# The second weight chunk between the modulation's two blocks, and two units begun on the first block

## The reference, cut to what matters

```python
c_act = jax.nn.silu(c)
for l in range(DEPTH):                                   # DEPTH = 2
    mod = c_act @ w_ada[l] + b_ada[l]                    # (1024) @ (1024, 3072)
    shift, scale, gate = jnp.split(mod, 3, axis=-1)
    h = rms_norm(x, norm_g[l]) * (1.0 + scale[:, None]) + shift[:, None]
    proj = h @ w_in[l]
    gq, gk, gv, glr, gz, dq, dk, dv, dz = split_columns(proj)
    gqkv = jax.nn.silu(causal_depthwise_conv(jnp.concatenate([gq, gk, gv], axis=-1), conv_w[l]))
    ...                                                  # two attention branches on these
    x = x + gate[:, None] * y
```

## Time and profile before

| | us |
|---|---|
| median of 3 runs (lowest, highest) | 1747.41 (1746.85, 1748.83) |
| the profiled execution | 1747.27 |
| its span | 1745.5 |
| PE busy | 1723.2 (99%) |
| ScalarE, VectorE, GpSimd busy | 672.0, 739.3, 732.1 |

### The profile page before, as it was taken

The page is one execution under the profiler, slowest core; times in us unless marked ns, Lnnn a source line. Parts: engine busy times, 40 slices in busy tenths (PEclk is TensorE's granted clock), DMA queues, the critical chain, the costliest instruction groups (busy, mean ns, idle before and its releaser), DMA issues.

```text
span 1745.5 us, 22025 instructions
## 1 busy us (share of the span) xinstructions
PE 1723.2 (99%) x8485; PEld 1407.4 (81%) x8485; DVE 739.3 (42%) x926; ACT 672.0 (38%) x871; POOL 732.1 (42%) x319
## 2 busy tenths in 40 slices
PE   6999999999999999999999999999999999999998
PEld 4677788777788888888889888888888888888887
DVE  4645765665766333332331634641113433333123
ACT  4444573544574433333333322232223333333223
POOL 1342226233225444444444444444444444444442
PEclk9999999999999999999999999999999999999999
DMA  9642115112113222222233322222222232222222
GB/s 356 236 145 97 49 49 217 49 73 97 49 49 116 101 96 96 96 89 78 90 105 111 109 95 96 96 97 97 96 96 96 75 115 96 98 97 75 85 98 82
DMA packets 34906, 180.75 MB, mean 104 GB/s; under 512 B 4470, under 2 KB 6652, under 8 KB 19356
## 3 DMA queue, kind: packets, MB, share of 16 engines
q1 hardware_dynamic: 28640, 161.50, 25.7%
q10 hardware_dynamic: 6204, 18.39, 2.9%
HBM read 177.78 MB, written 2.10 MB: 103 GB/s over the span
## 4 chain that ended last, share of the span: by engine, by line
issue 43%; PE 28%; POOL 25%; SPq 1%; DVE 1%; DMA 1%; ACT 1%; POOLq 0%; DVEq 0%; ACTq 0%
POOL wl_both L576 25%; PE ps L1123 4%; PE ps L1125 4%; PE ps L1124 4%; PE ps L1417 4%; PE ps L1419 3%; PE ps L1418 3%; SPq L521 1%; PE ps L1484 1%; PE ps L1458 1%; DMA ada_w<-w_ada 1%; PE ps L1259 1%; PE ps L1471 1%; PE ps L1495 0%; PE ps L1429 0%
## 5 line engine op out<-in xcount | busy, mean ns | idle before, releaser
L576 POOL TENSOR_TENSOR wl_both<-raw_both,wh_both 128x1024 fp32r<-128x1024 f32 (+1 forms) x256 | 609.5, 2401 | 733.4 <-ACT wh_both L668 731.0
L1123 PE MATMUL ps<-xh,wh_both 128*128 128x512 f32 x1280 | 503.1, 393 | 3.5 <-DVE xl L1956 1.6
L1125 PE MATMUL ps<-xh,wl_both 128*128 128x512 f32 x1280 | 498.4, 389 | 0.0
L1124 PE MATMUL ps<-xl,wh_both 128*128 128x512 f32 x1280 | 498.3, 389 | 0.0
L668 ACT ACTIVATE wh_both<-raw_both 128x2048 fp32r<-128x2048 f32 x127 | 243.4, 1916 | 494.4 <-PE ps L1125 484.3
L1123 PEld LDWEIGHTS ps<-xh,wh_both 128*128 128x128 f32 x1280 | 240.2, 188 | 65.9 <-issue 12.7
L1125 PEld LDWEIGHTS ps<-xh,wl_both 128*128 128x128 f32 x1280 | 240.2, 188 | 50.6
L1124 PEld LDWEIGHTS ps<-xl,wh_both 128*128 128x128 f32 x1280 | 240.4, 188 | 47.9
L598 POOL TENSOR_TENSOR wl_both<-raw_both,wh_both 128x1024 fp32r<-128x1024 f32 x46 | 113.3, 2477 | 238.9 <-ACT wh_both L823 167.0
L1123 PE MATMUL ps<-fh,wh_both 128*128 128x512 f32 (+1 forms) x374 | 141.2, 377 | 0.1
L1124 PE MATMUL ps<-fl,wh_both 128*128 128x512 f32 (+1 forms) x374 | 140.8, 376 | 0.0
(11 more groups left out here) (295 smaller groups left out, 2265.4 us busy)
## 6 DMA issues: line engine op xcount, KB each, us to landing
raw_both<-ffn_in_stream SPq DMA_DIRECT2D x44, 1024.0 KB, 4.7
raw_both<-mixer_stream SPq DMA_DIRECT2D x40, 1024.0 KB, 4.7
raw_both<-layer_stream SPq DMA_DIRECT2D x36, 1024.0 KB, 5.4
raw_both<-ffn_out_stream SPq DMA_DIRECT2D x32, 704.0 KB, 4.0
ada_late<-w_ada ACTq DMA_DIRECT2D x24, 512.0 KB, 4.5
ada_w<-w_ada SPq DMA_DIRECT2D x16, 512.0 KB, 12.2
gate_w<-w_ada ACTq DMA_DIRECT2D x4, 1024.0 KB, 11.4
x<-x_t SPq DMA_DIRECT2D x1, 2048.0 KB, 8.1
```

Of the source, the lines that this page charges most:

```text
L576: last = nc.gpsimd.tensor_tensor(wl[u][:, cols], raw[u][:, cols], wh[u][:, cols].bitcast(F32), ALU.subtract)
L1123: nc.tensor.matmul(bank_ap, w0, x0, start=first, stop=False)
L1124: nc.tensor.matmul(bank_ap, w0, x1, start=False, stop=False)
L1125: return nc.tensor.matmul(bank_ap, w1, x0, start=False, stop=last)
```

## The change

SP loads chunk 1 between block 0 and block 1 of the modulation, no longer after block 1. ScalarE takes chunk 1's high part after block 0's `xh`, no longer after block 1's, and issues `small_loads(1)` between the copy of block 1's rows and its `xh`, no longer after block 0's. PE runs unit 1 in the opening as well, in banks 2 and 7 (`SECOND_BANKS`): the slices 0 to 3 of both units stand between the tiles and transposes of block 1, the slices 4 to 7 of both behind them. Of the ten constant products around block 1's tiles (two, two and six) six remain, all ahead of unit 0. `late_tile(0)` waits until both banks of unit 1 are emptied, since bank 2 is its own; unit 2 waits for the banks of unit 0 instead of unit 1. ScalarE empties both tiles of unit 1 at its second quarter.

```diff
+SECOND_BANKS = (2, 7)
...
-            sp.dma_start(raw[1], ins["layer0_stream"][1]).then_inc(raw_landed[1], 16)
+                if b == 0:
+                    sp.dma_start(raw[1], ins["layer0_stream"][1]).then_inc(raw_landed[1], 16)
...
                         nc.scalar.activation(gate[:, b], ps[:, 4 + b], ACT.Copy).then_inc(rows_copied, 1)
+                        if b:
+                            small_loads(1)
...
                         if b == 0:
-                            small_loads(1)
-                        else:
                             take_high(first + 1)
...
-                    bank = ps[:, t]
+                    bank = ps[:, SECOND_BANKS[t] if (l, stage, j) == (0, "conv", 1) else t]
...
                         if kind in ("conv", "q"):
-                            if p % 2:
+                            if (l, kind, j) == (0, "conv", 1):
+                                for t in range(2 if p == 1 else 0):
+                                    empty(kind, j, t)
+                            elif p % 2:
                                 empty(kind, j, p // 2)
...
+            def second_steps(moving, low0, ks, tiles=(0, 1)):
+
+                for k in ks:
+                    pe.wait_ge(low_ready, low0 + k + 1)
+                    for t in tiles:
+                        if k == 0:
+                            half_ready(0, UNIT0["layer0"], 1, t)
+                        cols = slice((t * KT + k) * P, (t * KT + k + 1) * P)
+                        last = products(ps[:, SECOND_BANKS[t]], (wh[1][:, cols], wl[1][:, cols]),
+                                        (moving[0][:, k], moving[1][:, k]), k == 0, k == KT - 1)
+                        if k == KT - 1:
+                            last.then_inc(tile_done, 1)
...
                 pe.wait_ge(late_landed[buf], 16 * sum(loads))
+                if n == 0:
+                    pe.wait_ge(banks_free[1], emptied(1, 1))
...
                     ada_turn(0)
-                    constant_products(2)
-                    ada_tile(1, 0)
-                    constant_products(2)
+                    constant_products(6)
                     claim(0, unit0, 0)
                     chunk_ready(0, unit0, 0)
-                    first_steps(*first, range(0, 1))
+                    first_steps(*first, range(0, 2))
+                    ada_tile(1, 0)
+                    first_steps(*first, range(2, 4))
                     ada_tile(1, 1)
-                    first_steps(*first, range(1, 3))
+                    pe.wait_ge(mod_ready, 1)
+                    pe.wait_ge(xn_ready, KT)
+                    second_steps(*first, range(0, 4), (0,))
                     ada_tile(1, 2)
-                    first_steps(*first, range(3, 4), (0,))
                     ada_tile(1, 3)
-                    first_steps(*first, range(3, 4), (1,))
+                    second_steps(*first, range(0, 2), (1,))
                     ada_turn(1)
-                    constant_products(6)
+                    second_steps(*first, range(2, 4), (1,))
                     first_steps(*first, range(4, KT))
+                    second_steps(*first, range(4, KT))
...
+                    if (l, stage, j) == (0, "conv", 1):
+                        return
                     if stage in ("conv", "q"):
                         if half == 0:
-                            pe.wait_ge(banks_free[(unit - 1) % 2], emptied(unit - 1, t))
+                            emptied_by = unit - 2 if (l, stage, j) == (0, "conv", 2) else unit - 1
+                            pe.wait_ge(banks_free[emptied_by % 2], emptied(emptied_by, t))
```

## The result

The changed kernel takes 1753.21 us (median of 20 runs, 1749.84 to 1757.44), the kernel before 1747.61 (20 runs beside it, 1746.85 to 1749.18): a ratio of 1.0031, 95% interval 1.0025 to 1.0037. The forecast was 1749.6 with a range up to 1751.6; the change costs 5.6 us, not 2.2. The executions of the changed kernel don't scatter around one value, they lie in groups: one at 1749.84, 6 from 1750.3 to 1750.9, 3 from 1752.1 to 1752.4, 7 from 1754.0 to 1755.1, 3 from 1757.2 to 1757.4. The first profiled execution took 1752.20 us, 1750.5 of them its span.

A forecast was written before the change was run, and what follows sets the result against it. The prediction took TensorE, busy 99% of the span, as the bound. Unit 2 starting at 68.93 instead of 66.65 adds 2.3 us (1.6 gained by filling gaps, 3.85 paid for the wait) to 1747.27: 1749.6 us, range 1747.3 to 1751.6.

The forecast's parts named there:

- The timetable up to the stall: PE's opening, rebuilt from unit costs: first product at 27.78, `lr` at 56.24, 10.20 us later for 11.05 us of work.
- The moved transfer: Chunk 1 ahead of block 1 in SP's queue: 2.4 us delay per tile, costing nothing, with 1.7 us to spare.
- The wait and its price: PE behind `lr`, until ScalarE empties unit 1's banks: idle 3.85 us, whole kernel 2.3 us slower, 1749.6 us.
- the ledger's 68.93: Forecast start of unit 2 on PE: 63.96 plus late tiles and `gate`, against 66.65 before.
- where the ledger said 1.6: The same sum without PE's wait behind `lr`: 2.3 - 3.85, so 1.6 us faster than the kernel before.
- the clock falls in the new wait: Rival, PE's products behind the stall after `lr`: slow clock loses 1.75 us more, 1751.3 us; chance 0.18.
- the granted clock reads 9 in every slice: Argument from the profile before, tenths of full speed in every slice: speaks against any clock fall.
- this stretch is less than half as long: Argument against a clock fall: the 3.85 us stall compared with PE's idle stretch before 9.53 us.
- What PE does after about 70 us is untouched: PE's later work runs almost without gaps, so a shift at that point arrives whole at the end.
- Late load 4's slack: Load issued behind `gate`, landing at 77.2, asked for at 78.5: slack 1.3 us, nothing lost, up to 1 us possible.

The follow-up runs named there:

- the load alone: The kernel before with only chunk 1's load moved ahead of block 1's tiles in SP's queue: 1752.42 us, ratio 1.0025.
- the first trace of after: First profiled execution of the changed kernel, without any edit: 1752.20 us.
- The second extra trace: The changed kernel traced again without any edit, the second of two more traces: 1754.01 us.
- The other extra trace: The changed kernel traced again without any edit, the first of two more traces: 1756.52 us.
- the kernel with 32 calls: The changed kernel with 32 calls of the constant product, two products each, ahead of the first late tile's wait, filling 7.41 us: 1754.72 us, ratio 1.0041.
- those on banks 6 and 7: The changed kernel with unit 1 in banks 6 and 7, without the first late tile's wait: 1750.27 us; three kernels built further on it: 1748.64, 1746.70, 1744.79 us.
- the take of chunk 3 moved: The changed kernel with ScalarE's take of chunk 3's high part behind the copy of unit 1's second bank: 1750.25 us, ratio 1.0017.
- the second and third step: Banks 6 and 7, late load 2 early, plus block 1's last tiles earlier in the opening: 1746.70 us; besides, late load 4 right behind late load 3: 1744.79 us.
- the first step: The changed kernel with unit 1 in banks 6 and 7, no wait, and late load 2 issued with the first two, ahead of `lr`: 1748.64 us, ratio 1.0007.

## Why the prediction was wrong, by its own steps

**The timetable up to the stall: right.** First product 27.81 in the same timeline (27.78 forecast), block 1's transposes 42.02 (42.04), restart 45.12 (45.19) after 1.11 us of idle time (1.2), `lr` 56.13 (56.24), PE free 60.07 (60.11), stall 3.79 (3.85), end of the stall 63.86 (63.96). The moved transfer is hidden, no tile of block 1 waits; by the experiment on the load alone it is hidden by the products ahead of the tile, not by slack that was there: the prediction priced the delay at the last tile, and the one to price it at was the first.

**The wait and its price: right as a sum, in part by luck.** With the stall filled the kernel takes 1749.88, the forecast's 1749.6 within 0.3. Two errors nearly cancel in it: unit 2 starts at 68.50 there, 0.43 ahead of the ledger's 68.93, and late load 4 costs 0.74, which the sum had at nothing. With the wait removed and late load 2 issued early unit 2 starts 1.65 earlier than before, where the ledger said 1.6; here too the first product was 0.28 late with its x (28.06 against 27.78), so in the same timeline it is 1.9.

**The step that failed: the rival "the clock falls in the new wait", chance 0.18 and price 1.75 us.** The forecast put the clock's loss at nothing. It is the case in all three traced executions, and over the forecast it costs 1.1, 4.5 and 5.4 us in them (1.07, 1.07 + 3.4 and 1.07 + 4.31; 0.3 more each against the 1.92 us that the pair of late tiles takes at full clock). Which of the 20 executions have it is an estimate from their times and mean clocks; the sums of the three traces fit the groups so:

- 1749.6 + 1.07 (the loss in the first trace of after: unit 2 at 70.00, not 68.93) = 1750.7, near the group from 1750.3 to 1750.9. No trace of this group exists. Its mean granted clock is 0.998, and the traced execution with this loss has 0.999, so this sum may not be what happened in it.
- The same with the late chunk, 1.77 (5.14 - 3.37): 1752.4. The traced execution of 1752.20 is in that group; mean clock 0.999.
- 1749.6 + 1.07 + 3.4 = 1754.1. The second extra trace took 1754.01; the group of 7 has a mean clock of 0.996 to 0.997, so it too has a long stretch at half clock.
- 1749.6 + 1.07 + 4.31 (4.72 less the 0.41 ahead of the stall) + 1.4 for the chunk = 1756.4. The other extra trace took 1756.52; the last group, another 0.8 to 1.0 higher, has 0.994 to 0.995.
- The single execution at 1749.84 has a mean clock of 1.000 and lies at the forecast: without a fall, as far as its time and clock tell.

I set aside the clock on two grounds, and both were misread. First, "the granted clock reads 9 in every slice": a slice is 43.6 us, and 3.4 us at half clock leave 0.96 of it, which still prints as 9; that row could not speak against a fall. Nor could the windows at the start: where the constant products of the earlier trace rows are slow, from 9.5 us on, the granted clock of the kernel before reads 1.00 (11 products in this window, 19 of the same in the filled kernel's window from 60 to 62):

```profile
10.00:12.00 2.00, 2.00 (x11) 2.00 (x10) 1.61 (x3) 1.70 (x4) 0.00 (x0) 1.00 0.99 374
```

The pace was the better witness. Second, "this stretch is less than half as long" as the 9.5 us ahead of the first product: the runs show half clock behind idle times of 3.79, 3.74, 2.78, 2.45 and 1.99 us. (Not behind each of this size: waits of 1.78, 2.23 and 2.28 us, in the kernel with 32 calls and two of those on banks 6 and 7, have 1.00 in all windows behind them. And not only behind these: in two of the 14 traces the clock falls near 20 us behind 0.63 us. So the length of the last wait doesn't decide alone; what else does no run here shows.) And I priced the fall by one loss where it has a spread. (The loss itself was read a little high: 32 constant products take 3.84 us in this view, not 3.7, so 1.6 are lost in the earlier trace rows, not 1.75.)

That the fall at this place comes from the stall's idle time is shown from both sides: added alone to the kernel before, a stall of 3.74 us is followed by half clock and costs 5.9; filled with constant products it costs 3.6 (1751.09 against 1747.49), its length; filled in the changed kernel, it gives back 3.3 and shrinks the spread of the executions from 7.6 us to 1.4. How much of these medians is the clock and how much the late chunk is split in single traces only. The Trainium skill, "TensorE: Matmul & The Clock Gate", Part 1: The HAM clock gate, says that the slow state is the default and that an idle stretch brings back 1.2 GHz; the rows at 0.50 behind the stall in all three traces of the changed kernel agree, the three waits of 1.78 to 2.28 us named above don't show it, and the weight that the prediction gave to this rule was too small.

**The chunk near 540 us: not foreseen.** "What PE does after about 70 us is untouched" holds in the code. But the chunk that is awaited there lands 6.9 to 7.5 us after its issue instead of 4.8 (7.3 in the first trace of after), in 7 of the 14 traces of this study (this one of the changed kernel, its slower extra one, the load alone, the stall alone, and three of the four kernels on banks 6 and 7), and costs 1.4 to 1.8 us. In an eighth (the take of chunk 3 moved) it lands after 6.3 and PE doesn't wait for it. It goes neither with the fall of the clock behind a stall (two traces with such a fall lack it, two without one, those of the second and third step, have it) nor with a part of the change. None of the three traces with a filled stall has it; whether the filler keeps it away no run here shows. The one trace of the kernel before doesn't show it. Its cause stays open.

**Late load 4's slack.** I gave it 1.3 us by a landing of 4.5 us. With the stall filled its tile waits 0.74, and on banks 6 and 7 up to 2.28. The 4.5 is the median of single transfers, and a late load is two, issued one behind the other. With the stall filled the two are issued from 72.30 on and the tile starts at 78.92, 6.6 us later; in the first step it is 6.4 (70.64 to 77.00). So the term that was mis-sized is the landing of the whole load.

## What to carry to other kernels

A new wait on TensorE costs its own length, and then perhaps the clock: here the granted clock read 0.50 for 3 to 12 us behind waits of 1.99 to 3.79 us in seven traces, differently in each execution, and stayed at 1.00 behind waits of 2.23 and 2.28 in two others. So put work in a wait that is needed anyway, or constant products if there is none, or choose banks that need no wait; and look for the fall in windows of 1 or 2 us, since a page's slices hid 3.4 us of it. When PE's order is moved forward, move the loads behind it too, one by one, until no tile waits: here that, with two banks that need no wait and another order in the opening, made a loss of 5.6 us a gain of 3.0. And price a load of several transfers from its first issue to its last landing, not by one transfer's median.

## What was unexpected of the hardware

- Useless work made a kernel faster: 32 products of a constant, 3.84 us of them in a wait of that length, took 3.3 us off the median (a part of which can be the late chunk).
- The same program with the same stall of 3.79 us stays at half clock until about 67, 75 or 76 us in three executions.
- The granted clock reads 1.00 from 9.5 us on, while the first 32 constant products take 5.47 us instead of the 3.84 that 32 of them take at 60 us: at the start of the record the pace tells more than the clock's row.
- In two of the 14 traces the granted clock falls to 0.50 from about 20 to 23 us behind an idle time of 0.63 us, in code that is the same in the others, which have 1.00 there.
- A transfer of 512 KB that takes 4.5 us on the page's median took 4.9 and 5.9 us in a stretch where the queues moved 346 to 401 GB/s, so a late load of two, issued 0.4 us apart, took 6.3.
